# Shift and scale of the first norms: from row sums on VectorE, GpSimd and ScalarE to two-column matmuls on TensorE

## The reference

```python
sh1, sc1, g1, sh2, sc2, g2 = jnp.split(
    (jax.nn.silu(c) @ ada_w[layer] + ada_b[layer])[:, None, :], ADA_CHUNKS, axis=-1)
csh1, csc1, cg1, csh2, csc2, cg2 = jnp.split(
    jax.nn.silu(c_ctx) @ ada_w[layer] + ada_b[layer], ADA_CHUNKS, axis=-1)
h = modulate(rmsnorm(x, norm1_g[layer]), sh1, sc1)       # h * (1 + scale) + shift
hc = modulate(rmsnorm(ctx, norm1_g[layer]), csh1, csc1)
q, k, v, gu, gv, ga, gb = jnp.split(h @ w, IN_SPLITS, axis=-1)
k_c, v_c = jnp.split(hc @ w[:, NA_WIDTH:3 * NA_WIDTH], 2, axis=-1)
```

## Time and profile before

| | us |
|---|---|
| median of 3 runs | 3052.77 |
| lowest and highest | 3045.84, 3053.87 |
| the profiled execution | 3046.86 |
| its span, first to last instruction | 3044.8 |
| PE busy in it | 2885.1 (95%) |
| DVE, POOL, ACT busy | 1395.4, 1160.6, 1054.5 |
| mean granted TensorE clock | 0.972 |

### The profile page before, as it was taken

The page is one execution under the profiler, slowest core; times in us unless marked ns, Lnnn a source line. Parts: engine busy times, 40 slices in busy tenths (PEclk is TensorE's granted clock), DMA queues, the critical chain, the costliest instruction groups (busy, mean ns, idle before and its releaser), DMA issues.

```text
span 3044.8 us, 38949 instructions
## 1 busy us (share of the span) xinstructions
PE 2885.1 (95%) x13052; PEld 2335.9 (77%) x13096; DVE 1395.4 (46%) x2486; ACT 1054.5 (35%) x1683; POOL 1160.6 (38%) x481
## 2 busy tenths in 40 slices
PE   3989998999999999999999999999898999899998
PEld 2778776888888888887888888886674688688886
DVE  8247332199925555542555555555217621311101
ACT  3144323333345555543222222223213332322221
POOL 5204443344543333334444444443330154344442
PEclk7989999999999999999999999999997899999999
DMA  6225422244454454456666676664220033223221
GB/s 231 69 104 212 158 89 84 83 148 147 143 171 166 182 195 165 162 212 191 193 193 193 193 193 193 192 193 135 69 88 11 22 110 97 76 92 97 96 95 55
DMA packets 252992, 418.70 MB, mean 138 GB/s; under 512 B 149760, under 2 KB 151168, under 8 KB 250592
## 3 DMA queue, kind: packets, MB, share of 16 engines
q1 hardware_dynamic: 227952, 372.03, 38.5%
q10 hardware_dynamic: 23488, 37.76, 3.4%
q0 software_dynamic: 1456, 7.73, 0.7%
HBM read 346.42 MB, written 69.99 MB: 137 GB/s over the span
## 4 chain that ended last, share of the span: by engine, by line
PE 92%; DVE 4%; issue 2%; ACT 1%; DMA 0%; ACTq 0%; DVEq 0%; SPq 0%
PE bank L993 27%; PE bank L995 27%; PE bank L994 27%; PE bank L1217 2%; PE bank L1206 2%; PE bank L1034 1%; DVE T L1423 1%; PE bank L1092 1%; DVE rr L1419 1%; PE bank L1079 1%; PE bank L1069 1%; PE bank L1317 0%; PE bank L1335 0%; PE bank L1171 0%; DVE ada L1440 0%
## 5 line engine op out<-in xcount | busy, mean ns | idle before, releaser
L545 POOL TENSOR_TENSOR wlo<-wraw,whi 128x1024 fp32r<-128x1024 f32 x456 | 1127.1, 2472 | 1678.6 <-ACT whi L617 1678.5
L993 PE MATMUL bank<-HH,whi 128*128 128x512 f32 x2160 | 873.2, 404 | 76.2 <-DVE HL L1434 50.3
L995 PE MATMUL bank<-HH,wlo 128*128 128x512 f32 x2160 | 846.3, 392 | 0.0
L994 PE MATMUL bank<-HL,whi 128*128 128x512 f32 x2160 | 844.2, 391 | 0.0
L617 ACT ACTIVATE whi<-wraw 128x1024 fp32r<-128x1024 f32 x456 | 482.4, 1058 | 923.3 <-PE bank L995 833.5
L993 PEld LDWEIGHTS bank<-HH,whi 128*128 128x128 f32 x2160 | 408.3, 189 | 176.5 <-issue 75.6
L995 PEld LDWEIGHTS bank<-HH,wlo 128*128 128x128 f32 x2160 | 407.7, 189 | 88.3
L994 PEld LDWEIGHTS bank<-HL,whi 128*128 128x128 f32 x2160 | 408.4, 189 | 85.3 <-issue 0.2
L1738 DVE TENSOR_TENSOR WL<-AJ,WH 128x512 fp32r<-128x512 f32 x128 | 313.4, 2449 | 333.3 <-ACT WH L864 333.3
L993 PE MATMUL bank<-WH,whi 128*128 128x512 f32 x1024 | 398.4, 389 | 2.8 <-DVE WL L1738 2.8
L994 PE MATMUL bank<-WL,whi 128*128 128x512 f32 x1024 | 398.3, 389 | 0.0
(11 more groups left out here) (256 smaller groups left out, 2819.9 us busy)
## 6 DMA issues: line engine op xcount, KB each, us to landing
wraw<-in_w SPq DMA_DIRECT2D x456, 512.0 KB, 3.6
act_dram<-actb ACTq DMA_DIRECT2D x128, 256.0 KB, 2.9
gate_dram<-GS SPq DMA_DIRECT2D x8, 4096.0 KB, 13.1
AJ<-act_dram SPq DMA_DIRECT2D x128, 256.0 KB, 2.7
GJ<-gate_dram SPq DMA_DIRECT2D x128, 256.0 KB, 3.7
adaw<-in_ada SPq DMA_DIRECT2D x32, 512.0 KB, 5.4
ada<-in_ada SPq DMA_DIRECT2D x16, 512.0 KB, 14.1
NB<-in_nab POOLq DMA_DIRECT2D x4, 1024.0 KB, 5.1
```

Source lines behind the costliest of these rows:

```text
L545: nc.gpsimd.tensor_tensor(wlo[:, slot, :, :].rearrange("p k c -> p (k c)"), wraw[:, slot, :, :].rearrange("p k c -> p (k c)"), whi[:, slot ...
L993: pe.matmul(out_, ah, bh, start=first, stop=False, **kw)
L994: pe.matmul(out_, ah, bl, start=False, stop=False, **kw)
L995: return pe.matmul(out_, al, bh, start=False, stop=last, **kw)
```

## The change

The 2048 first sums come from PE. The host lays the first 2048 columns of `ada_w` out as 16 tiles whose rows are input features, so that each 128x128 block can be a weight of a matmul; `c` and `c_ctx` come as `cc`, 128 partitions of 8 blocks of two numbers. For each of the 16 output blocks PE adds up eight fp32 matmuls with two columns, 128 in all, into 32 columns of PSUM bank 6; the norm sum of X stands behind the fourth tile. DVE first makes X times the reciprocal root (T), then adds the bias to all 32 columns at once, makes both gains, and then goes block by block: scale and shift in one operation, and the low part of the block before. ACT's high part needs no shift any more. The row sums of the first 16 tiles, POOL's products and ACT's copies are gone, and so is everything for the context behind HL. SP puts the loads of weight tiles 0 and 1 ahead of ada tiles 8 and 12. The loads of the later ada tiles wait for the evacuation of v, since PE's sums no longer count in `ada_used`; a `load_ada` stands behind the copies of v in SP's queue in both kernels.

```diff
@@ sync
-            sp.dma_start(sc2[:, :, :], bass.AP(tensor=A["c"].tensor, offset=0, ap=[[0, P], [D, 2], [1, D]])).then_inc(c_in, 16)
+            sp.dma_start(cc[:, :, :], A["cc"]).then_inc(c_in, 16)
             for dst, src in ((X[:, :, :], A["x"]), (cols[:, :], A["cols"]), (ones[:, :], A["ones"])):
                 sp.dma_start(dst, src).then_inc(const_in, 16)
             for a in range(16):
-                sp.dma_start(ada1[:, a, :], A["ada"][a, :, :]).then_inc(ada1_in[a], 16)
+                if a in (8, 12):
+                    g = (a - 8) // 4
+                    load_w(g, g, peeled=True)
+                sp.dma_start(ada1[:, a, :], A["ada1"][a, :, :]).then_inc(ada1_in[a], 16)
...
             def load_ada(a, slot):
-                sp.wait_ge(ada_used, a - R + 1)
-                sp.dma_start(adaw[:, slot, :], A["ada"][a, :, :]).then_inc(ada_in[slot], 16)
+                if isinstance(a, int) and a < 16 + R:
+                    sp.wait_ge(tile_evac, G0["gu"])
+                else:
+                    sp.wait_ge(ada_used, a - (16 + R - 1))
+                sp.dma_start(adaw[:, slot, :], A["ada"][a - 16, :, :]).then_inc(ada_in[slot], 16)
...
-            for g in range(R):
+            for g in range(2, R):
                 load_w(g, g, peeled=True)
@@ gpsimd
-            pool.wait_ge(silu_c, 1)
-            for a in range(KB):
-                pool.wait_ge(ada_used, a + 1)
-                nc.gpsimd.tensor_tensor(ada1[:, a, :], ada1[:, a, :], sc2[:, 1, :], ALU.mult).then_inc(ada_mul, 1)
@@ scalar
-            nc.scalar.activation(sc2[:, :, :], sc2[:, :, :], ACT.Silu).then_inc(silu_c, 1)
+            nc.scalar.activation(cc[:, :, :], cc[:, :, :], ACT.Silu).then_inc(silu_c, 1)
...
-            act.wait_ge(gsc_ready, 1)
-            norm_apply(S, lambda kb: mod[:, kb, 0:1], HH)
+            norm_apply(S, None, HH)
...
-            for a in range(KB):
-                act.wait_ge(ada_mul, a + 1)
-                nc.scalar.activation(ada1[:, a, :], ada1[:, a, :], ACT.Copy, accum_out=mod[:, a, 1:2])\
-                    .then_inc(ada_ctx, 1)
@@ tensor
             pe.wait_ge(const_in, CONST0)
-            norm_sum(S)
+            pe.wait_ge(silu_c, 1)
+            for a in range(16):
+                if a == 4:
+                    norm_sum(S)
+                pe.wait_ge(ada1_in[a], 16)
+                for kb in range(KB):
+                    mm = pe.matmul(bank[6][:, 2 * a:2 * a + 2], ada1[:, a, kb * P:(kb + 1) * P], cc[:, kb, :],
+                                   start=(kb == 0), stop=(kb == KB - 1))
+            mm.then_inc(ada_done, 1)
@@ vector
-            v.wait_ge(silu_c, 1)
-            for a in range(16):
-                if a == 11:
-                    norm_rstd(S)
-                v.wait_ge(ada1_in[a], 16)
-                if a >= 2:
-                    v.wait_ge(ada_used, a - 1)
-                row_sum(ada1[:, a, :], sc2[:, 0, :], junk[:, a % 2, :], a, 0).then_inc(ada_used, 1)
-            v.wait_ge(ada_used, 16)
-            add_bias(0, 16, 0)
-            gain_scale(0, 8, 0, "n1")
-            v.wait_ge(gsc_ready, 1)
-            norm_scale(X, S, lambda kb: gsc[:, 0, kb:kb + 1])
-            norm_low(S, HH, HL, lambda kb: mod[:, kb, 0:1])
-            for a in range(KB, 16):
-                ins = row_sum(ada1[:, a, :], sc2[:, 1, :], ada1[:, a, :], a, 1)
-            then(ins)
-            v.wait_ge(ada_ctx, KB)
-            add_bias(0, 16, 1)
-            gain_scale(1, 8, 1, "n1")
+            norm_rstd(S)
+            for kb in range(KB):
+                nc.vector.tensor_tensor(T[:, kb, :], X[:, kb, :], rstd, ALU.mult).then_inc(n_rows, 1)
+            v.wait_ge(ada_done, 1)
+            a = COLS["adab"][0]
+            then(nc.vector.tensor_tensor(mod[:, 0:16, :], bank[6][:, 0:32].rearrange("p (a w) -> p a w", w=2),
+                                         bc(cols[:, a:a + 16], 2, 2), ALU.add))
             gain_scale(0, 8, 0, "n1")
+            gain_scale(1, 8, 1, "n1")
+            v.wait_ge(gsc_ready, 2)
+            for kb in range(KB + 1):
+                if kb < KB:
+                    v.wait_ge(n_rows, kb + 1)
+                    nc.vector.tensor_scalar(T[:, kb, :], T[:, kb, :], gsc[:, 0, kb:kb + 1], mod[:, kb, 0:1], ALU.mult,
+                                            ALU.add).then_inc(n_scaled, 1)
+                if kb:
+                    v.wait_ge(n_hi, kb)
+                    nc.vector.tensor_tensor(HL[:, kb - 1, :], T[:, kb - 1, :], HH[:, kb - 1, :].bitcast(F32),
+                                            ALU.subtract).then_inc(n_lo, 1)
```

More of the change, by code:

```diff
@@ L116, in build @@
         mod = sb("mod", [P, 48, 2])
+        cc = sb("cc", [P, KB, 2])
         gsc = sb("gsc", [P, 3, KB])
@@ L154, in build @@
         CX = a3("CX", [P, KB, CTX])
[L155 to L159, removed]
         CH = a3("CH", [P, KB, CTX], FR)
@@ L285, in build @@
         ada_used = sem("ada_used")
-        ada_mul = sem("ada_mul")
-        ada_ctx = sem("ada_ctx")
+        ada_done = sem("ada_done")
+        n_rows = sem("n_rows")
         c_in = sem("c_in")
@@ L428, in _ @@
         def _(sp):
-            sp.dma_start(sc2[:, :, :], bass.AP(tensor=A["c"].tensor, offset=0, ap=[[0, P], [D, 2], [1, D]])).then_inc(c_in, 16)
-            for dst, src in ((X[:, :, :], A["x"]), (cols[:, :], A["cols"]), (ones[:, :], A["ones"])):
-                sp.dma_start(dst, src).then_inc(const_in, 16)
-            for a in range(16):
-                sp.dma_start(ada1[:, a, :], A["ada"][a, :, :]).then_inc(ada1_in[a], 16)
-            def load_ada(a, slot):
-                sp.wait_ge(ada_used, a - R + 1)
-                sp.dma_start(adaw[:, slot, :], A["ada"][a, :, :]).then_inc(ada_in[slot], 16)
             def load_w(g, slot, peeled=False):
@@ L446, in load_w, with load_ada @@
                     .then_inc(w_in[slot], 16)
+            sp.dma_start(cc[:, :, :], A["cc"]).then_inc(c_in, 16)
+            for dst, src in ((X[:, :, :], A["x"]), (cols[:, :], A["cols"]), (ones[:, :], A["ones"])):
+                sp.dma_start(dst, src).then_inc(const_in, 16)
+            for a in range(16):
[3 more added lines that the diff above has]
+                sp.dma_start(ada1[:, a, :], A["ada1"][a, :, :]).then_inc(ada1_in[a], 16)
+            def load_ada(a, slot):
+                if isinstance(a, int) and a < 16 + R:
[3 more added lines that the diff above has]
+                sp.dma_start(adaw[:, slot, :], A["ada"][a - 16, :, :]).then_inc(ada_in[slot], 16)
             sp.dma_start(CX[:, :, :], A["ctx"]).then_inc(ctx_in, 16)
@@ L1454, in _ @@
             nc.vector.memset(eps[:, :], EPS).then_inc(n_eps, 1)
-            v.wait_ge(silu_c, 1)
-            for a in range(16):
-                if a == 11:
-                    norm_rstd(S)
-                v.wait_ge(ada1_in[a], 16)
-                if a >= 2:
-                    v.wait_ge(ada_used, a - 1)
-                row_sum(ada1[:, a, :], sc2[:, 0, :], junk[:, a % 2, :], a, 0).then_inc(ada_used, 1)
-            v.wait_ge(ada_used, 16)
-            add_bias(0, 16, 0)
-            gain_scale(0, 8, 0, "n1")
-            v.wait_ge(gsc_ready, 1)
-            norm_scale(X, S, lambda kb: gsc[:, 0, kb:kb + 1])
-            norm_low(S, HH, HL, lambda kb: mod[:, kb, 0:1])
-            for a in range(KB, 16):
-                ins = row_sum(ada1[:, a, :], sc2[:, 1, :], ada1[:, a, :], a, 1)
-            then(ins)
-            v.wait_ge(ada_ctx, KB)
-            add_bias(0, 16, 1)
-            gain_scale(1, 8, 1, "n1")
+            norm_rstd(S)
[5 more added lines that the diff above has]
+                                         bc(cols[:, a:a + 16], 2, 2), ALU.add))
+            gain_scale(0, 8, 0, "n1")
+            gain_scale(1, 8, 1, "n1")
+            v.wait_ge(gsc_ready, 2)
[8 more added lines that the diff above has]
+                                            ALU.subtract).then_inc(n_lo, 1)
+            scaled[2] += KB
             def copy_tile(g, dst, src):
@@ L1567, in _ @@
             ada_rows(32, 48)
-            v.wait_ge(ada_used, 48)
+            v.wait_ge(ada_used, 32)
             add_bias(16, 32, 0)
@@ L2022, in pack @@
         w=pack_tiles(inp),
-        ada=inp["ada_w"][0].T.reshape(48, P, D),
+        ada=inp["ada_w"][0][:, 16 * P:].T.reshape(32, P, D),
+        ada1=inp["ada_w"][0][:, 0:16 * P].reshape(KB, P, 16, P).transpose(2, 1, 0, 3).reshape(16, P, D),
+        cc=np.stack([inp["c"][0], inp["c_ctx"].reshape(D)]).reshape(2, KB, P).transpose(2, 1, 0),
         x=feature_rows(inp["x"][0]), ctx=feature_rows(inp["ctx"][0]),
-        c=np.stack([inp["c"][0], inp["c_ctx"].reshape(D)]),
+        c=inp["c"],
         cols=np.concatenate([tables[n] for n in COLS], 1), ones=np.ones((P, P), f), ident=np.eye(P, dtype=f),
```

## The result

| us | before | after |
|---|---|---|
| median of 7 runs each, one chip | 3048.59 | 3059.30 |
| lowest and highest | 3045.84, 3053.87 | 3057.36, 3064.27 |
| the profiled execution | 3046.86 | 3059.77 |
| its span | 3044.8 | 3057.6 |
| mean granted TensorE clock | 0.972 | 0.970 |

The ratio is 1.0035, with a 95% interval of 1.0024 to 1.0047: the change makes the kernel slower, by 10.7 us between the medians. Four more runs of the kernel before moved its own median from the 3052.77 that the prediction started from to 3048.59, so the absolute forecast (3063.5) stands 4.2 us too high, and the difference is the +10.7 that was summed.

The account below looks back on a forecast made before the run. PE was taken to bound the kernel, busy 95% of the span. The terms 13.9+1.7-3.2-1.7 gave +10.7 us, so 3063.5 us from the median of 3052.77; the range was 3044 to 3068.

Parts of the forecast that it names:

- full clock kept behind it: PE's stream behind the norm sum: full clock lasts 2.0 us, in which 18 loads go.
- hand-over to q: Between the stream's end and q: handing over, bias, gains, scale, high and low part take 2.9 us.
- q's first tile: First q projection tile: DVE's two operations per block, 1.13 us, make it 8.6 us instead of 6.9, +1.7.
- wait for CL: PE ahead of k: the 3.21 us wait goes, as DVE is done at 26.3 us from q's start, k's earliest 28.6.
- The load's price: PE's new stream: each of 256 weight loads takes 0.216 us at low clock, 0.108 at full clock.
- The clock: PE's stream behind the norm sum: the remaining 174 loads go at low clock, 37.6 us, ending at 72.4.
- first rival: PE's stream: full clock or a clock-independent load price all through, stream end 46.6, -15.1 us, 3037.7; chance 0.15.
- What ran beside the stream: DVE's reciprocal and eight products for X, 3.3+5.3 us or up to 23, end before 72.4, hidden by the stream.
- The context: Context norm ahead of k: PE's wait goes, -3.2 us, and the low clock behind it, -1.65.
- the second: PE's stream: slow for four tiles, woken by the norm sum and kept up, end 53.5, -8.2 us, 3044.6; chance 0.10.
- The third: PE's stream: low clock but loads at 0.165 us, end 60.3, -1.4 us, 3051.4; chance 0.12.
- The fourth: The forecast, but PE stays slow through q's first tile and the stream loses its 2 us: about +14, 3067; inside forecast's spread.

Follow-up runs that it names:

- e1: The changed kernel with 128 columns per small matmul instead of two, the same 256 loads; median 3036.05 us against 3048.43 before, ratio 0.9958.
- e8: The changed kernel with the norm sum of X ahead of the first tile instead of behind the fourth; 3060.0 us in one run.
- e4: The changed kernel with input blocks 4 to 7 left out of every sum, 128 loads instead of 256; 3030.79 us in one run.
- e6: The changed kernel with DVE's old batch order, all eight scales first, then all eight low halves; 3062.59 us in one run.
- e7: The changed kernel with weight tiles 0 and 1 loaded behind all 16 ada tiles, as before; 3058.01 us in one run.
- e5: The kernel before, without POOL's eight products and ACT's eight copies, DVE making all 16 context sums; 3051.91 us against 3049.25, ratio 1.0007.
- e2: The changed kernel with 64 columns per small matmul instead of two, into two PSUM banks; 3044.9 us in one run.
- e3: The changed kernel with one column per small matmul instead of two, the context's sums left out; 3057.91 us in one run.
- e9: The changed kernel with 128 columns, PE making blocks 0 to 9, DVE 10 to 15, norm sum first; 3031.51 us against 3048.94 before, ratio 0.9941.

## Why the prediction was right, step by step

The sum gave +10.7 us; the medians differ by 10.7, and the profiled starts of the attentions by 10.1 and 10.0. The terms as the traces have them (+13.9 for q's start, +1.3 for its first tile, -3.2 and -1.65 for the context) give 10.3.

| term | forecast | trace |
|---|---|---|
| stream starts | 9.9 | 10.73 |
| first 64 loads | 13.8 | 13.6 |
| norm sum | 9.1 | 9.7 |
| full clock kept behind it | 2.0 | 2.7 |
| stream ends | 72.4 | 72.6 |
| hand-over to q | 2.9 | 2.6 |
| q starts | 75.2 | 75.21 |
| q's first tile | 8.6 | 8.3 |
| wait for CL | none | none |

That the stream's end came out within 0.2 us is in part luck. It began 0.8 us late and the norm sum took 0.6 longer, so that the later part started at 34.06 and not at 32.8; and it took 38.5 us instead of 39.6, since the clock was kept longer and a load cost 0.213 and not 0.216.

**The load's price** was the step with the widest bounds, 0.165 to 0.22 at low clock. The measured 0.213 is twice the 0.112 at full clock less 5%. The reasoning by doubling from L1171 and from the norm sum's records held roughly, and 0.216 came so close because the 0.108 that was doubled was itself a little low; the 0.16 us between two loads of a cold start, rightly left as a bound, didn't hold.

**The clock** decided, and it was the step with least to stand on: a stretch from 2315 to 2335 us with small matmuls and 0.55, against one from 200 to 240 with 1.00. The stretch at 0.55 had gaps (13.69 us busy of 20) and the new stream has none, so the row that it was ranked with matched it in the small matmuls only, and the other one, at 1.00, in the lack of gaps; that the choice fell on the right one was in part luck. It came out at 0.50 in a gapless stream, and e1 shows that the thin matmuls make the difference: with 128 columns the same loads ran at 1.00 and the time fell by 23 us, to 3036.1, where the first rival (full clock all through) had 3037.7. The Trainium skill, page "TensorE: Matmul & The Clock Gate", section "Why this matters for your kernels", tells to keep TensorE continuously busy to hold full clock. Here it was busy for 36.00 of 36.00 us at 0.50, and in e8 for another 49 us: being busy was not enough, and the measurement decides. The same page's "LDWEIGHTS (loading the stationary operand)" prices a load at its columns over 1.2 in nanoseconds, 107 for 128; that agrees with 0.112 us at full clock and is half of what was measured at the low one.

**What ran beside the stream** was hidden as forecast. X times the root took 9.20 us, part of it beside POOL, inside the bounds of 5.3 and 19.6, and DVE idled 23.71 us behind it. e4 shows the other side: with the stream 30 us shorter nothing else was late.

**q's first tile.** The +1.7 us were put on DVE's per-block pace of 1.13 us, which gave 8.6. The trace has 8.3 where before had 7.0, so +1.3, and by another limit: the step was close in size and wrong in its reason. There were 13 matmuls at the low clock where before had seven, six more at 0.2 us each (0.43 instead of 0.23 apart), and e6 shows the same 8.4 without the per-block order. DVE's pace was real, 1.06 us a block, and gives 7.9 when the clock rises earlier (e7). The prediction carried the old tile's seven slow matmuls over unchanged, and that number isn't fixed: seven before the change and in e7, 12 in e5, 13 in the change, in e6 and in e8. The per-block order in itself pays: it starts q 2.6 us earlier.

**The context.** No wait for CL, and no low clock ahead of k, as summed (-3.2 and -1.65). But CL was done 27.5 us behind q's start and not 26.3, since its scales took 4.65 us beside POOL instead of 3.26, and PE came to k 28.1 us behind q's start, so the margin was 0.6 us and not 2.3. An estimate from these rows: one more such stretch of 1.4 us would have brought back a wait of 0.8.

**Rivals.** The first and the second came to be as kernels, e1 and e2, once the matmuls were 128 and 64 columns wide. They were priced at 3037.7 and 3044.6 on a median of 3052.77; measured were 3036.05 and 3044.9 beside a median of 3048.43, so they gained 12.4 and 3.5 us where 15.1 and 8.2 were summed. The third, 0.165 us a load at low clock, no run shows. The fourth came in part: PE stayed slow through 13 of the 24 matmuls of q's first tile, but the stream didn't lose its time at full clock, and the 8.6 us that were put down to DVE cover what these cost.

## What to carry to other kernels

Before work moves onto the engine that bounds a kernel, count its instructions at the lower clock too, and see whether its matmuls are wide beside their weight loads: 256 loads with two columns took 52 us of PE's time, and repeating the columns until each had 128 brought them down to 30.6, with no time lost by the added columns. Idle time of PE ahead of a first result is free for such work only up to the point at which it would come out even: a stream that ends at 61.7 us by the prediction's sum, at 57 to 62 by the ends and times of the runs. So split the work with the engine that did it before, and keep POOL's two-operand work off DVE's stretch: in these runs it made DVE's operations two to three times as long in most of the places where they met.

## What the runs showed of the hardware

- An fp32 matmul stream without a gap was granted 1.2 GHz for 36 us (49 in e8) with one or two columns per matmul. With 64 columns it kept, for 21.5 us, the 2.4 GHz that a dense sum had reached; from a cold start it stayed at the slow spacing for 13.9 us. With 128 columns it came to the fast spacing 3.5 us behind a cold start. Where between these numbers the behaviour changes no run shows.
- The granted clock reads 1.00 from the start of each of these traces, also where the loads' spacing of 0.213 us is that of 1.2 GHz (10 to 24 us in the change).
- Behind a dense sum the thin stream kept full clock for 2.7 us in the change and in e8, and for 4.7 to 4.9 in e3, e7 and e4; e7 has the same code on PE as the change. So two kernels with the same work may differ by 2 to 3 us here.
- A load of 128 fp32 columns started every 0.112 us at 2.4 GHz and every 0.213 at 1.2; 64 of them took 13.79, 13.78 and 13.89 us with one, two and 64 columns behind each.
- DVE operations stretched beside POOL's fp32 tensor_tensor: a row sum from 1.23 to 3.36 us (e9), eight scales from 5.39 to 11.66 (e5), eight products from 4.90 (e9, no POOL beside them) to 9.20 (after), and two TENSOR_SCALAR, which read one tensor only, from 1.00 to 3.15 (e9).
- Not always is it DVE that stretches. In e6 POOL's tensor_tensor at 79.16 us took 4.93 us instead of 2.40, and DVE's eight low halves beside it took 4.90, as eight such operations do alone. DVE's reciprocal kept its 3.35 us beside POOL (e9, 31.14 to 34.49).
